# Output projection of a two-layer decoder step: its low parts and squares in a new order, and sixteen cached pages asked for ahead of the sliding branch's rows

## The chip, the core and the metric

The kernel runs on one core of a Trainium2 chip. The time is the device time of one execution in microseconds (us). The kernel before took 1862.92 us, the median of 3 runs (1859.42 to 1864.6). Everything is computed in one launch, in float32, most matmuls as products of float32 split in two parts.

## The reference, cut to what matters

Two groups of tokens share the weights: a prompt of 512 tokens, and 8 sequences of 4 new tokens each (32 tokens), with cached keys and values. All 544 tokens pass through 2 layers. Cut to the stages that the change touches:

```python
def window_attn(q, kv, q_pos, k_pos): ...        # sliding branch: the last 512 positions
def nsa_cmp_sel(q, cm, sb, q_pos): ...           # compressed branch, and 16 selected blocks of 64

def trunk_layer(x, c, pos, conv_buf, attend, recur, lw):
    ...
    q = rope(a_q...)
    kv_c, kv_s, kv_w = make_kv(a_kc, pos), make_kv(a_ks, pos), make_kv(a_kw, pos)
    o_c, o_s, o_w, win_state = attend(q, kv_c, kv_s, kv_w)
    a_out = gate[0] * o_c + gate[1] * o_s + gate[2] * o_w
    h, mstate = recur(mq, mk, mv, ...)
    m_out = sigmoid(m_o) * rms(h)
    x = x + g1 * (concatenate([a_out, m_out]) @ wo)        # the output projection
    xn2 = rmsnorm(x, n2) * (1 + sc2) + sh2                 # needs the squares of all of x
    f, new_buf = conv_ffn(xn2, conv_buf, w_up, ...)
    return x + g2 * f, ...
```

For the 8 sequences, past_s = cache_sel_kv[l][page_table] is 8 pages of 128 positions a sequence (64 pages a layer, 128 KB each), and cache_win_kv[l] holds 512 positions a sequence (512 KB each). The window rows, moved on by 4 positions, are outputs too.

## The kernel before, in words

Every engine has one queue of instructions in program order. They meet at semaphores (`sig(...)`: a producer adds 1, a consumer waits for a count), and all of TensorE, VectorE, ScalarE and GpSimd meet twice a layer at a fence, the semaphore `stage_done`: each adds 1 and waits until all four have.

**Decode attention** (between fence 8 and fence 12). SyncE issues the loads in one queue. In `pages` (L545 and L546) it reads a page's number from on-chip memory and then issues the DMA of that page. The pages of sequences 0 to 5 go first. It then waits for `mx_t` (TensorE has turned the last gates, L970), issues the window rows of sequences 0 to 3 (L598), the 16 pages of sequences 6 and 7, and the window rows of sequences 4 to 7. TensorE handles this in six rounds (`ROUNDS`, four sequences and 512 positions each): selected blocks of sequences 0 to 3 (rounds 0, 1), of 4 to 7 (rounds 2, 3), window rows of 0 to 3 (round 4) and of 4 to 7 (round 5). In `turn_keys` (L1027) it transposes keys; VectorE and ScalarE copy them out of PSUM, `score` (L1039) multiplies them by the queries, and the softmax and the values (L1078) follow. Where the pages of sequences 6 and 7 are turned is the second half of round 2. GpSimd waits for each half of the window rows and then stores them to the output (`put`, L2421), 8 stores a half; later it loads the recurrent state (L2487), and after VectorE has added to that state (`state_added`, L2227) it stores it by four pairs of DMAs (L2421 and L2499). It adds to `stage_done` after the last of these.

**Output projection** (after fence 12). `w_out` is loaded into `slab[0]` (output columns 0 to 511) and `slab[1]` (512 to 1023). ScalarE copies a slab, rounded, to `hiO` (`split_out`, L1579), and VectorE leaves the remainder in the slab (`low_out`, in place, L1721). The activations are split in the same way (`hiX` by ScalarE at L1593, the remainder `xnT` by VectorE). TensorE takes 8 chunks of 128 output columns. A chunk is 48 matmuls at L1192 (8 slices of the contraction, three products, two halves of the tokens). VectorE adds each chunk to the residual stream (`residual`, L2259 to L2264), ScalarE squares it (`square`, L1327), and TensorE sums the squares (`norm_sum`, L636): those of chunk 0 after the matmuls of chunk 1, and so on. Three pairs of PSUM banks hold chunks, so chunk c waits until chunk c-3 has been added.

VectorE's order there is: the remainder of `slab[0]`, the fence, 8 remainders of the activations, the remainder of `slab[1]`, the remainder of the first slice of the FFN's up weights (`split_w(0, 0)`, `slab[2]`), and only then the 8 additions. ScalarE's is: `hiX`, the copy of `slab[1]`, a wait for `slab[2]` and `split_w(0, 0)` (L1601), and then the 8 squares. After the last chunk the norm's root is taken and the FFN starts with the slice that `split_w(0, 0)` has prepared.

Of the kernel before, what the change touches and what calls it, by code (L numbers as in the profile page):

```python
# [125 lines left out]
def trunk_program(nc, A, O):  # L126
# [10 lines left out]
    with ctx:  # L137
# [197 lines left out]
        sig = Signal  # L335
# [30 lines left out]
        def slab_loads(stage, i, L, j=0):  # L366

            s, m = i % NSLAB, PARTS[stage]
            return L * (16 * dmas[s]) + j * (16 * m) + 16 * (first_dma[stage, s] + m * (i // NSLAB + 1))
# [118 lines left out]
        def x_at(k):  # L488

            return k + 1 if k < 4 else k + 2  # L490
        d_hi, d_lo = sig("weights_high", 2 + 2 * (NG + 1)), sig("weights_low", 2 + 2 * (NG + 1))
        i_hi, i_lo, i_lo0 = sig("input_weights_high", N_SLAB_IN), sig("input_weights_low", N_SLAB_IN - 1), sig("first_input_weights_low", 4)
        y_acc, y_add = sig("down_accumulated", 8 * (NG + 1)), sig("down_added", 8 * (NG + 1), credit=2)
        ul_t, ul_c = sig("tail_transposed", 6), sig("tail_copied", 6)
# [23 lines left out]
        def _(sp):  # L518
# [22 lines left out]
            for L in range(DEPTH):  # L541
# [50 lines left out]
                for b in range(6):  # L592
                    if b % 2 == 0:
                        sp.wait_ge(mod_t.sem, mod_t.at(mod_last(L, (1, 2, 0)[b // 2]) + 1))
                    pages(spg[b], sel_pool, b, spg_in[b // 2])
                sp.wait_ge(mx_t.sem, mx_t.at(4, L))
                for b in range(NB):
                    sp.dma_start(wpg[b].rearrange("p i c -> p (i c)"),  # L598
                                 A["cache_win_kv"][L][b].rearrange("(p i) a k d -> p (i a k d)", i=4)).then_inc(wpg_in[b // 4], 16)
                    if b == 3:  # L600
                        for c in (6, 7):
                            pages(spg[c], sel_pool, c, spg_in[c // 2])
                for i in range(2):
                    cols = slice(512 * i, 512 * i + 512)
                    load("out", i, [(sl(i, 8, 512)[:, 4:8, :], wout[L, :, 4:8, cols])] +
# [20 lines left out]
        def _(pe):  # L626
# [72 lines left out]
            for L in range(DEPTH):  # L699
# [477 lines left out]

                for c in range(8):
                    i = c // 4
                    if c % 4 == 0:  # L1180
                        pe.wait_ge(d_lo.sem, d_lo.at(i + 1, L))
                    if c >= 3:
                        pe.wait_ge(o_add.sem, o_add.at(c - 2, L))
                    cc = 128 * (c % 4)
                    lo = slab[i][:, :].rearrange("p (k n) -> p k n", k=8)
                    for k in range(KC):
                        if c == 0:
                            pe.wait_ge(x_lo.sem, x_lo.at(X_OUT + k + 1, L))
                        wh, wl = fr(hiO[i][:, k, cc:cc + 128]), fr(lo[:, k, cc:cc + 128])
                        for n, (wt, x) in enumerate(((wh, hiX), (wh, xnT), (wl, hiX))):  # L1190
                            for b in range(2):
                                ins = mm(ps[2 * (c % 3) + b][:, 0:HALF], wt, fr(x[:, k, HALF * b:HALF * b + HALF]),  # L1192
                                         start=k == 0 and n == 0, stop=k == KC - 1 and n == 2)
                                if c == 4 and k == 0 and n == 0 and b == 0:
                                    ins.then_inc(slab_out[0], 1)
                    ins.then_inc(o_acc.sem, 1)
                    if c:
                        norm_sum(2 * L + 1, c - 1, frees=1 if c == 7 else None)
                    if c == 5:
                        history()  # L1200
# [45 lines left out]
                def down(n_k, g=0, last=False):  # L1246

                    pe.wait_ge(h_lo.sem, h_lo.at(n_k + 4 * g, L))
                    pe.wait_ge(d_lo.sem, d_lo.at(4 + 2 * g, L))
                    lo = slab[1][:, :].rearrange("p (k n) -> p k n", n=D)  # L1250
                    for c in range(8):
                        pe.wait_ge(y_add.sem, y_add.at(c - 1 + 8 * g, L))
                        bank = (0 if last else 4) + 2 * (c % 2)
                        for k in range(n_k):
                            wh, wl = fr(hiD[:, k, 128 * c:128 * c + 128]), fr(lo[:, k, 128 * c:128 * c + 128])
                            for n, (wt, x) in enumerate(((wh, hiH), (wh, hid), (wl, hiH))):
                                for b in range(2):
                                    ins = mm(ps[bank + b][:, 0:HALF], wt, fr(x[:, k, HALF * b:HALF * b + HALF]),  # L1258
                                             start=k == 0 and n == 0, stop=k == n_k - 1 and n == 2)
                                    if last and c == 0 and k == 0 and n == 0 and b == 0:  # L1260
                                        ins.then_inc(slab_out[2], 1)
                        ins.then_inc(y_acc.sem, 1)
                        if last:
                            if c == 0:
                                pe.wait_ge(y_add.sem, y_add.at(8 * g, L))
                            if c < 6:
                                tail_rows(c)
                            if c >= 2:
                                norm_sum(2 * L + 2, c - 2)
                    pe.drain().then_inc(slab_out[1], 1)  # L1270
                    if last:
                        norm_sum(2 * L + 2, KC - 2)
                        norm_sum(2 * L + 2, KC - 1)
                        spread(2 * L + 2)
# [43 lines left out]
        def _(act):  # L1318
# [54 lines left out]
            for L in range(DEPTH):  # L1373
# [226 lines left out]
                        act.wait_ge(g_acc.sem, g_acc.at(cd - 1, L))  # L1600
                    A_(fr(hiU[:, q % 2, :, :, :]), src[:, :, :, cc:cc + 128], ACT.Copy).then_inc(w_hi.sem, 1)  # L1601

                act.wait_ge(slab_in[2], slab_loads("ffn", 2, L))
                split_w(0, 0, False)
                for c in range(8):
                    act.wait_ge(o_add.sem, o_add.at(c + 1, L))
                    square(2 * L + 1, c)
                root(2 * L + 1)

                def u_chunk(s, cd):  # L1610
# [60 lines left out]
        def _(dve):  # L1671
# [91 lines left out]
            for L in range(DEPTH):  # L1763
# [476 lines left out]
                state_added(4)  # L2240
                dve.wait_ge(d_out.sem, d_out.at(1, L))
                cp(xnT[:, 0:4, SEQ:TT], ps[6][:, 0:128].rearrange("p (g t) -> p g t", g=AG))
                state_added(5)

                def low_out(i):
                    dve.wait_ge(d_hi.sem, d_hi.at(i + 1, L))
                    low(slab[i][:, :].rearrange("p (k n) -> p k n", k=8), hiO[i]).then_inc(d_lo.sem, 1)

                low_out(0)
                dve.drain().then_inc(stage_done, 1)  # L2250
                dve.wait_ge(stage_done, stage_end(12, L))

# [13 lines left out]
                for k in range(KC):  # L2266
                    dve.wait_ge(x_hi.sem, x_hi.at(X_OUT + k + 1, L))
                    low(xnT[:, k, :], hiX[:, k, :]).then_inc(x_lo.sem, 1)
                low_out(1)

                def split_w(q, cd):
                    src = slab[(2, 0)[q % 4 // 2]][:, :].rearrange("p (k h n) -> p k h n", k=8, h=2)
# [1 line left out]
                    dve.wait_ge(w_hi.sem, w_hi.at(cd + 1, L))  # L2274
                    low(src[:, :, :, cc:cc + 128], hiU[:, q % 2, :, :, :]).then_inc(w_lo.sem, 1)

                split_w(0, 0)
                norm_scales(112 + 8 * L, 32)
                for c in range(8):
                    dve.wait_ge(o_acc.sem, o_acc.at(c + 1, L))  # L2280
                    residual(c, ps[2 * (c % 3)], ps[2 * (c % 3) + 1], 16 + c).then_inc(o_add.sem, 1)
                    drain()
                    if c == 6:
                        dve.wait_ge(cv_t.sem, cv_t.at(1, L))
                        cp(convS[:, :, :].rearrange("p c n -> p (c n)"), ps[7][:, 0:16 * FC])
                        dve.wait_ge(win_kept, 3 * L + 2)
                        V.memset(up[:, :, 0:2], 0.0)
# [264 lines left out]
```

## Time and profile before

| what | value |
|---|---|
| median of 3 runs | 1862.92 us (1859.42 to 1864.6) |
| the profiled execution's own time | 1863.74 us |
| its span in the trace | 1861.6 us |
| mean granted TensorE clock | 0.941 of full speed |
| TensorE busy | 1712.3 us (92%) |
| VectorE, ScalarE, GpSimd busy | 916.4 us (49%), 610.9 us (33%), 193.0 us (10%) |

TensorE is busy nearly all the time, so that what matters is where it stands still, and where it runs at the lower clock. A row of the timeline gives start and length of a group of instructions, and in brackets how long the engine had been idle and what released it. The chain of waits follows the end of the kernel back through what released what. SPq is SyncE's queue of DMA issues, L636 a line of kernel.py.

### The profile page before, as it was taken

The numbers are of one execution on the slowest core, as the hardware profiler recorded it, in microseconds if no ns is written. First come the engines' busy times: TensorE is split into PE (matmuls) and PEld (weight loads), VectorE is DVE, ScalarE is ACT, GpSimd is POOL, SyncE is SP. The second block draws the span as 40 slices with busy tenths as digits, with TensorE's granted clock in tenths as the row PEclk, the third lists the DMA queues.
The fourth block names the chain that finished last, engine by engine and source line by source line (L and its number), as shares of the span: only waits on it lengthen the run. The fifth ranks groups of instructions, "written<-read, shape, count | busy, mean of one in ns | idle before, by whom it ended". The sixth has DMA issues, their size and how long they took to land.

```text
span 1861.6 us, 37154 instructions
## 1 busy us (share of the span) xinstructions
PE 1712.3 (92%) x14719; PEld 1537.6 (83%) x14719; DVE 916.4 (49%) x2362; ACT 610.9 (33%) x1165; POOL 193.0 (10%) x312
## 2 busy tenths in 40 slices
PE   5899999976989999999989999897788999999996
PEld 4899875555889999999989997645588999999995
DVE  2444434645355645555463343474534655545643
ACT  2422225633133324224152212563323422412313
POOL 1001003433000000000000100153300000000001
PEclk9899978987989999999999997898888999999998
DMA  8335368379212222221123535635831222321201
GB/s 294 118 99 179 99 234 267 109 229 210 59 46 91 91 91 90 90 70 65 49 83 90 178 101 192 213 98 163 218 79 46 91 91 71 110 76 60 90 23 53
DMA packets 154291, 218.97 MB, mean 118 GB/s; under 512 B 11722, under 2 KB 112394, under 8 KB 153964
## 3 DMA queue, kind: packets, MB, share of 16 engines
q1 hardware_dynamic: 145872, 197.12, 33.3%
q0 software_dynamic: 8288, 20.04, 4.1%
q8 instruction: 89, 1.46, 0.3%
q14 instruction: 42, 0.34, 0.1%
HBM read 200.45 MB, written 16.68 MB: 117 GB/s over the span
## 4 chain that ended last, share of the span: by engine, by line
PE 80%; SPq 5%; DMA 5%; DVE 4%; ACT 3%; issue 2%; POOL 0%; DVEq 0%; ACTq 0%
PE ps L1232 27%; PE ps L1258 14%; PE ps L803 13%; PE ps L1192 4%; DMA slab<-in_w_up 4%; PE ps L677 3%; SPq L545 2%; SPq L546 2%; PE ps L848 1%; PE ps L914 1%; PE ps L884 1%; PE ps L789 1%; PE ps L798 1%; PE ps L797 1%; PE ps L929 1%
## 5 line engine op out<-in xcount | busy, mean ns | idle before, releaser
L1232 PE MATMUL ps<-work_r,big_r 128*128 128x272 f32 x1344 | 279.2, 289 | 5.6 <-issue 5.3
L1232 PE MATMUL ps<-work_r,slab_r 128*128 128x272 f32 x1344 | 278.5, 288 | 0.0
L1232 PE MATMUL ps<-xnT_r,big_r 128*128 128x272 f32 x1344 | 276.5, 287 | 0.0
L1232 PEld LDWEIGHTS ps<-work_r,big_r 128*128 128x128 f32 x1344 | 210.1, 188 | 8.1 <-issue 8.1
L803 PE MATMUL ps<-slab_r,work_r 128*128 128x256 f32 (+1 forms) x976 | 213.3, 285 | 0.0
L1232 PEld LDWEIGHTS ps<-xnT_r,big_r 128*128 128x128 f32 x1344 | 211.7, 188 | 0.0
L1232 PEld LDWEIGHTS ps<-work_r,slab_r 128*128 128x128 f32 x1344 | 210.6, 188 | 0.0
L1721 DVE TENSOR_TENSOR slab_r<-slab,big_r 128x2048 fp32r<-128x2048 f32 (+2 forms) x72 | 168.9, 2349 | 59.3 <-ACT big_r L1601 51.6
L803 PEld LDWEIGHTS ps<-slab_r,work_r 128*128 128x128 f32 x976 | 163.3, 191 | 2.7 <-issue 2.5
L1619 ACT ACTIVATE big<-big,work 128x560 f32<-128x560 f32 x44 | 33.6, 764 | 371.0 <-DVE big L2311 371.0
L1258 PE MATMUL ps<-side_r,big_r 128*128 128x272 f32 x704 | 148.3, 292 | 4.9 <-DVE big_r L1721 4.9
L1258 PE MATMUL ps<-big_r 128*128 128x272 f32 x704 | 146.2, 289 | 0.0
L1258 PE MATMUL ps<-side_r,slab_r 128*128 128x272 f32 x704 | 146.1, 289 | 0.0
L2259 DVE TENSOR_TENSOR work<-ps,modT 128x32 f32<-128x32 f32 x112 | 21.4, 191 | 252.1 <-PE ps L1258 180.6
L2421 POOL DMA_DIRECT2D out<-work x32 | 18.2, 574 | 1073.4 <-ACT work L1657 815.2
L1258 PEld LDWEIGHTS ps<-side_r,big_r 128*128 128x128 f32 x704 | 111.1, 190 | 7.7 <-DVE big_r L1721 5.4
L1258 PEld LDWEIGHTS ps<-big_r 128*128 128x128 f32 x704 | 111.5, 190 | 0.0
L1258 PEld LDWEIGHTS ps<-side_r,slab_r 128*128 128x128 f32 x704 | 111.0, 190 | 0.0
L1601 ACT ACTIVATE big_r<-slab 128x2048 fp32r<-128x2048 f32 x44 | 84.3, 1917 | 65.3 <-PE ps L1232 52.9
L803 PE MATMUL ps<-work_r 128*128 128x256 f32 (+1 forms) x336 | 96.4, 287 | 0.0
L803 PE MATMUL ps<-work_r,xnT_r 128*128 128x256 f32 (+1 forms) x336 | 94.1, 280 | 0.0
L803 PE MATMUL ps<-slab_r,xnT_r 128*128 128x256 f32 x320 | 90.8, 284 | 0.0
(447 smaller groups left out, 3232.6 us busy)
## 6 DMA issues: line engine op xcount, KB each, us to landing
slab<-in_w_mod SPq DMA_DIRECT2D x23, 2048.0 KB, 9.1
slab<-in_w_up SPq DMA_DIRECT2D x44, 1024.0 KB, 7.5
slab<-in_w_in SPq DMA_DIRECT2D x20, 1024.0 KB, 5.6
slab<-in_w_down SPq DMA_DIRECT2D x20, 1024.0 KB, 5.9
slab<-in_cache_cmp_kv SPq DMA_DIRECT2D x128, 128.0 KB, 2.0
slab<-in_cache_sel_kv SPq DMA_DIRECT2D x96, 128.0 KB, 2.0
big<-in_cache_win_kv SPq DMA_DIRECT2D x16, 512.0 KB, 5.1
out<-big POOLq DMA_DIRECT2D x16, 448.0 KB
```

The costliest lines, as they stand in the source:

```text
L545: pg = sp.value_load(pages_sb[0:1, NPG * b + p:NPG * b + p + 1], min_val=0, max_val=N_PHYS - 1)
L546: sp.dma_start(dst[:, p, :], src[bass.ds(pg + L * N_PHYS, 1)].squeeze(0)).then_inc(sem, 16)
L677: ins = mm(bank[32 * q:32 * q + 32, 0:128], cT[:, k, :], wv[:, k, 128 * q:128 * q + 128], start=k == 0, stop=k == KC - 1, tile_position=(0 ...
L789: ins = mm(ps[t][:, 0:cw], x, fr(wt[:, k, :]), start=k == 0 and m == 0, stop=k == KC - 1 and m == 2)
L803: ins = mm(ps[n % 4][:, 0:cw], x, fr(wt[:, k, :]), start=k == 0 and m == 0, stop=k == KC - 1 and m == 2)
L1192: ins = mm(ps[2 * (c % 3) + b][:, 0:HALF], wt, fr(x[:, k, HALF * b:HALF * b + HALF]), start=k == 0 and n == 0, stop=k == KC - 1 and n == 2)
L1232: ins = mm(ps[2 * half + b][:, 0:HALF], wt, fr(x[:, k, HALF * b:HALF * b + HALF]), start=k == 0 and n == 0, stop=k == KC - 1 and n == 2)
L1258: ins = mm(ps[bank + b][:, 0:HALF], wt, fr(x[:, k, HALF * b:HALF * b + HALF]), start=k == 0 and n == 0, stop=k == n_k - 1 and n == 2)
L1601: A_(fr(hiU[:, q % 2, :, :, :]), src[:, :, :, cc:cc + 128], ACT.Copy).then_inc(w_hi.sem, 1)
L1619: A_(cv[:, s, 0:UPW - 2], cv[:, s, 0:UPW - 2], ACT.Silu, bias=cbias[:, s:s + 1]).then_inc(u_si.sem, 1)
L1721: return tt(fr(dst), dst, fr(hi).bitcast(F), ALU.subtract)
L2259: tt(tmp.rearrange("p (b t) -> p b t", b=NB), hi[:, SEQ - HALF:HALF].rearrange("p (b t) -> p b t", b=NB), bc(gs, 2, NT), ALU.mult)
```

## The change

Three things are edited.

- SyncE: the 16 pages of sequences 6 and 7 are issued before all eight window rows (before: after the first four).
- The remainder of `w_out` is made in eight pieces of 128 columns instead of two of 512. Only the first stands ahead of the fence, and ahead of the last `state_added`. Three follow the activations, two each follow the additions of chunk 0 and chunk 1. TensorE waits for a piece ahead of every chunk; the counts of `weights_low` are moved by 6 for this.
- `split_w(0, 0)` goes on ScalarE behind the square of chunk 4, and on VectorE behind the addition of chunk 5.

```diff
@@ block.sync
                 sp.wait_ge(mx_t.sem, mx_t.at(4, L))
+                for c in (6, 7):
+                    pages(spg[c], sel_pool, c, spg_in[c // 2])
                 for b in range(NB):
                     sp.dma_start(wpg[b]...).then_inc(wpg_in[b // 4], 16)
-                    if b == 3:
-                        for c in (6, 7):
-                            pages(spg[c], sel_pool, c, spg_in[c // 2])
@@ block.tensor
-                    if c % 4 == 0:
-                        pe.wait_ge(d_lo.sem, d_lo.at(i + 1, L))
+                    pe.wait_ge(d_lo.sem, d_lo.at(c + 1, L))
@@ block.scalar
-                act.wait_ge(slab_in[2], slab_loads("ffn", 2, L))
-                split_w(0, 0, False)
                 for c in range(8):
                     act.wait_ge(o_add.sem, o_add.at(c + 1, L))
                     square(2 * L + 1, c)
+                    if c == 4:
+                        act.wait_ge(slab_in[2], slab_loads("ffn", 2, L))
+                        split_w(0, 0, False)
@@ block.vector
+                def low_out(i, cols):
+                    dve.wait_ge(d_hi.sem, d_hi.at(i + 1, L))
+                    low(slab[i]...[:, :, cols], hiO[i][:, :, cols]).then_inc(d_lo.sem, 1)
+
+                low_out(0, slice(0, 128))
                 state_added(5)
-                low_out(0)
                 dve.drain().then_inc(stage_done, 1)
@@
                     low(xnT[:, k, :], hiX[:, k, :]).then_inc(x_lo.sem, 1)
-                low_out(1)
+                for c in range(1, 4):
+                    low_out(0, slice(128 * c, 128 * c + 128))
@@
-                split_w(0, 0)
                 norm_scales(112 + 8 * L, 32)
                 for c in range(8):
                     residual(c, ...).then_inc(o_add.sem, 1)
                     drain()
+                    for n in ((0, 1), (2, 3))[c] if c < 2 else ():
+                        low_out(1, slice(128 * n, 128 * n + 128))
+                    if c == 5:
+                        split_w(0, 0)
```

VectorE's queue around fence 12 and behind it, before (the wait for `stage_done` is the fence; `slab_r<-slab,big_r` is a remainder of weights, `out_accumulated` a finished chunk):

```order
L2242 COPY xnT<-ps 128x4x32 [waits dec_out]
L2227 TENSOR_TENSOR work<-work,ps 128x2x129 [waits dec_state_sums]
L1721 TENSOR_TENSOR slab_r<-slab,big_r 128x4096 [waits weights_high]
L1721 TENSOR_TENSOR xnT_r<-xnT,work_r 128x544 [waits inputs_high,stage_done]
L1721 TENSOR_TENSOR xnT_r<-xnT,work_r 128x544 [waits inputs_high] x7
L1721 TENSOR_TENSOR slab_r<-slab,big_r 128x4096 [waits weights_high]
L1721 TENSOR_TENSOR slab_r<-slab,big_r 128x16x128 [waits up_w_high]
L1744 SCALAR_TENSOR_TENSOR scale_n<-modT,colsA 128x72
L2259 TENSOR_TENSOR work<-ps,modT 128x32 [waits out_accumulated]
```

and in the changed kernel (its line numbers are lower by one here):

```order
L2241 COPY xnT<-ps 128x4x32 [waits dec_out]
L1720 TENSOR_TENSOR slab_r<-slab,big_r 128x8x128 [waits weights_high]
L2226 TENSOR_TENSOR work<-work,ps 128x2x129 [waits dec_state_sums]
L1720 TENSOR_TENSOR xnT_r<-xnT,work_r 128x544 [waits inputs_high,stage_done]
L1720 TENSOR_TENSOR xnT_r<-xnT,work_r 128x544 [waits inputs_high] x7
L1720 TENSOR_TENSOR slab_r<-slab,big_r 128x8x128 [waits weights_high] x3
L1743 SCALAR_TENSOR_TENSOR scale_n<-modT,colsA 128x72
L2258 TENSOR_TENSOR work<-ps,modT 128x32 [waits out_accumulated]
```

A remainder of 4096 columns ahead of the fence became one of 1024, and it now precedes the last state addition; behind the fence the addition of chunk 0 no longer has the wait for `up_w_high` (the split of the up weights) ahead of it.

ScalarE's queue from the copy of `slab[1]` on, before:

```order
L1579 ACTIVATE big_r<-slab 128x4096 [waits slab1_loaded]
L1601 ACTIVATE big_r<-slab 128x2048 [waits slab2_loaded]
L1327 ACTIVATE big<-xT 128x544 [waits out_added] x2
L1327 ACTIVATE big<-xT 128x544 [waits norm_sums_spread,out_added] x6
L1332 ACTIVATE rstd<-rstd 128x136 [waits norm_var_inverse_scaled]
```

and in the changed kernel:

```order
L1577 ACTIVATE big_r<-slab 128x4096 [waits slab1_loaded]
L1325 ACTIVATE big<-xT 128x544 [waits out_added] x2
L1325 ACTIVATE big<-xT 128x544 [waits norm_sums_spread,out_added] x3
L1599 ACTIVATE big_r<-slab 128x2048 [waits slab2_loaded]
L1325 ACTIVATE big<-xT 128x544 [waits norm_sums_spread,out_added] x3
```

The wait for the load of `slab[2]` moved from ahead of all squares to behind five of them.

## Rows read from the trace of the kernel before

**Rows 1.** The page: the chain's shares by engine

```profile
PE 80%; SPq 5%; DMA 5%; DVE 4%; ACT 3%; issue 2%; POOL 0%; DVEq 0%; ACTq 0%
```

**Rows 2.** Chain of waits, layer 0's output projection (start, length, what)

```profile
439.75 34.16 DMA slab<-in_w_up
...
473.94 1.93 ACT big_r L1601
...
475.89 2.29 DVE slab_r L1721
...
480.66 7.73 PE ps L1192 x48
...
488.76 6.23 PE ps L1192 x48
```

**Rows 3.** Chain of waits, layer 1, the same chunk

```profile
1370.87 8.42 PE ps L1192 x48
```

**Rows 4.** Timeline of TensorE: first matmul, and first sum of squares of both layers

```profile
461.61 0.79 PE L1192 MATMUL ps<-work_r,big_r 128*128 128x272 f32 x2 [6.11 <-DVE xnT_r L1721]
...
480.22 0.44 PE L636 MATMUL ps<-big,shape_constants 128*32 128x136 f32 x8 [3.54 <-ACT big L1327]
...
1370.19 0.68 PE L636 MATMUL ps<-big,shape_constants 128*32 128x136 f32 x8 [4.96 <-ACT big L1327]
```

**Rows 5.** TensorE by microsecond: stretch, length, busy, clock, DMA share, GB/s

```profile
482.00:483.00 1.00, 1.00 (x6) 0.50 0.00 0
```

**Rows 6.** Timeline of VectorE around fence 12, layer 0

```profile
454.08 0.29 DVE L2242 COPY xnT<-ps 128x128 f32<-128x128 f32 x1 [0.88 <-PE ps L1115]
455.14 0.42 DVE L2227 TENSOR_TENSOR work<-work,ps 128x258 f32<-128x258 f32 x1 [0.77 <-PE ps L1105]
455.48 4.42 DVE L1721 TENSOR_TENSOR slab_r<-slab,big_r 128x4096 fp32r<-128x4096 f32 x1
460.74 5.17 DVE L1721 TENSOR_TENSOR xnT_r<-xnT,work_r 128x544 fp32r<-128x544 f32 x8 [0.84 <-ACT work_r L1593]
```

**Rows 7.** Timeline of GpSimd around fence 12, layers 0 and 1

```profile
455.86 0.69 POOL L2421 DMA_DIRECT2D out<-work  x1 [3.65 <-DVE work L2227]
...
459.26 0.69 POOL L2499 DMA_DIRECT2D out<-work  x1
...
1348.72 0.69 POOL L2499 DMA_DIRECT2D out<-work  x1
```

**Rows 8.** Timeline of SyncE's queue, layer 0

```profile
385.78 1.85 SPq L598 DMA_DIRECT2D big<-in_cache_win_kv  x4
388.73 19.51 SPq L546 DMA_DIRECT2D big<-in_cache_sel_kv  x16
408.28 1.86 SPq L598 DMA_DIRECT2D big<-in_cache_win_kv  x4
```

**Rows 9.** Line L545, 385 to 412 us: ns min/median/max, first and last start

```profile
L545 SPq TENSOR_LOAD <-pages_sb x16: 265/272/1626, 387.7 to 407.2; - x16
```

**Rows 10.** Timeline of TensorE: rounds 2 (layers 0, 1) and 5 (layer 0)

```profile
410.06 1.09 PE L1027 MATMUL ps<-shape_constants,big 128*128 128x128 f32 x8 [1.78 <-DMA big<-in_cache_sel_kv]
...
421.81 1.07 PE L1027 MATMUL ps<-shape_constants,big 128*128 128x128 f32 x8 [0.93 <-ACT work L1545]
...
1300.10 1.09 PE L1027 MATMUL ps<-shape_constants,big 128*128 128x128 f32 x8 [1.43 <-DMA big<-in_cache_sel_kv]
```

**Rows 11.** Timeline of GpSimd, layer 0: stores of the window rows, loads of state

```profile
395.83 4.23 POOL L2421 DMA_DIRECT2D out<-big  x8 [3.77 <-issue]
416.64 4.16 POOL L2421 DMA_DIRECT2D out<-big  x8 [16.58 <-DMA big<-in_cache_win_kv]
428.46 2.79 POOL L2487 DMA_DIRECT2D work<-in_state_mlstm_C  x4 [7.66 <-PE ps L1039]
```

**Rows 12.** Engines by stretch: length, busy of five, clock, DMA share, GB/s

```profile
388.00:392.00 4.00, 4.00 (x76) 3.15 (x76) 1.30 (x10) 0.87 (x5) 3.98 (x9) 0.66 0.99 367
...
420.00:424.00 4.00, 3.08 (x27) 1.79 (x25) 2.70 (x4) 2.27 (x4) 0.80 (x2) 1.00 0.98 305
```

More of the change, by code:

```diff
@@ L490, in x_at @@
             return k + 1 if k < 4 else k + 2
-        d_hi, d_lo = sig("weights_high", 2 + 2 * (NG + 1)), sig("weights_low", 2 + 2 * (NG + 1))
+        d_hi, d_lo = sig("weights_high", 2 + 2 * (NG + 1)), sig("weights_low", 8 + 2 * (NG + 1))
         i_hi, i_lo, i_lo0 = sig("input_weights_high", N_SLAB_IN), sig("input_weights_low", N_SLAB_IN - 1), sig("first_input_weights_low", 4)
@@ L1248, in down @@
                     pe.wait_ge(h_lo.sem, h_lo.at(n_k + 4 * g, L))
-                    pe.wait_ge(d_lo.sem, d_lo.at(4 + 2 * g, L))
+                    pe.wait_ge(d_lo.sem, d_lo.at(10 + 2 * g, L))
                     lo = slab[1][:, :].rearrange("p (k n) -> p k n", n=D)
@@ L2242, in _ @@
                 cp(xnT[:, 0:4, SEQ:TT], ps[6][:, 0:128].rearrange("p (g t) -> p g t", g=AG))
+                def low_out(i, cols):
+                    dve.wait_ge(d_hi.sem, d_hi.at(i + 1, L))
+                    low(slab[i][:, :].rearrange("p (k n) -> p k n", k=8)[:, :, cols], hiO[i][:, :, cols]).then_inc(d_lo.sem, 1)
+                low_out(0, slice(0, 128))
                 state_added(5)
-                def low_out(i):
-                    dve.wait_ge(d_hi.sem, d_hi.at(i + 1, L))
-                    low(slab[i][:, :].rearrange("p (k n) -> p k n", k=8), hiO[i]).then_inc(d_lo.sem, 1)
-                low_out(0)
                 dve.drain().then_inc(stage_done, 1)
```

## The prediction, made before the changed kernel was run

> **What bounds the kernel now.** I began with the page: the chain that ended last is TensorE for 80% [rows 1], so an edit pays where TensorE stands still or runs slowly. I then read the chain of waits through the output projection, and after it TensorE's timeline for every idle time there.
>
> The chain leaves TensorE for the load of the first up weights, which lands at 473.9 us; then follow ScalarE's copy, VectorE's remainder until 478.2, and chunk 0's addition and square [rows 2]. TensorE has done chunks 0 and 1 by then and stands still before it can sum chunk 0's squares, 3.54 us in layer 0 and 4.96 us in layer 1 [rows 4]. Nothing that it waits for needs the up weights: they only stand ahead in two queues. Behind the pause TensorE's granted clock is 0.50 for some microseconds [rows 5], that is 1.2 of 2.4 GHz, so the next chunk takes 7.73 and 8.42 us in place of 6.23 [rows 2, 3].
>
> The second place is fence 12, which was passed at about 460 us. VectorE reaches it at 455.48 + 4.42 = 459.90 [rows 6]. GpSimd's last issue ends at 459.26 + 0.69 = 459.95 [rows 7], and only then does it add to the fence. They tie. In layer 1 GpSimd's last issue ends at 1349.41 [rows 7].
>
> The third is round 2 of the decode attention: TensorE waits 1.78 us and 1.43 us for the pages of sequences 6 and 7 [rows 10]. SyncE issues these behind four window rows (1.85 us), and takes 19.51 us over them, the last at 408.2 [rows 8].
>
> **Squares and up-weight split.** The order of events afterwards, in layer 0 and in today's times: TensorE ends chunk 1 at 480.22 - 3.54 = 476.7, so chunk 0 ends 6.23 us earlier, at 470.4. VectorE is done with the activations at 460.74 + 5.17 = 465.9 [rows 6]. It then has three pieces of 1024 columns. No row has that shape. The nearest are 2.29 us for 2048 columns, cut the same way [rows 2], and 4.42 for 4096 whole [rows 6]; the difference is 2.13 for 2048, so 1.1 to 1.2 by proportion, and 2.29 as the upper bound (a piece as dear as one of twice the size). I take 1.2. The pieces end at 467.1, 468.3 and 469.5, and chunk 1 needs the first of them at 470.4. Addition and square of chunk 0 take from 478.24 to 480.2 today, about 2 us, and end at 472.5, 4 us before they are needed. Even with 2.29 a piece they end at 475. So the pause goes whole: 3.54 + 4.96 = 8.50 us. With it goes the slow chunk: (7.73 - 6.23) + (8.42 - 6.23) = 3.69 us, since nothing interrupts TensorE between chunks 0 and 1 any more. Sum 12.19; bounds: 8.50 if the lower clock comes anyway at another place, 12.5 with the slower sums beside it.
>
> What is late next? The four pieces of slab 1 stand behind additions 0 and 1: 4 x 1.2 (9.2 at the bound) within two chunks of 6.23, and chunk 4 needs the first of them only three chunks later. The up weights are split behind square 4, after 495 us, when they have long landed; VectorE's 2.29 stand between additions 5 and 6, in a gap of one chunk. Nothing of this reaches TensorE. Chunk 4's release of slab 0 moves earlier with everything else.
>
> **The remainder ahead of the fence.** It shrinks from 4.42 to 1.2, but GpSimd hides all of this gain: its six issues (three pairs, 455.86 to 459.95 [rows 7]) begin 0.30 us after the last state addition, which ended at 455.56 [rows 6]. That addition now stands behind the piece. The copy ends at 454.37, the piece follows until about 455.5, and the addition starts at 455.45 instead of 455.14. The fence comes 0.3 us later, 0.6 for both layers; with a piece of 2.29 it is 1.4 a layer, 2.8 in all. With the pieces free it would be zero.
>
> A page has a rule on this spot. The Trainium skill, SBUF — State Buffer, says in the warning on DVE blocking DMA that the descriptors of a DMA issued by GpSimd are written through ports that it shares with VectorE, so that some VectorE operations hold it up. A shorter remainder could then speed up GpSimd's issues too. The rows don't show that: each issue takes 0.69 us beside the long remainder.
>
> **Pages ahead of the window rows.** SyncE starts on the pages at once, 1.9 us earlier. Today the last issue ends at 408.24 [rows 8] and TensorE goes on 1.8 us later [rows 10]. 1.9 us earlier is just in time for its wish, 410.06 - 1.78 = 408.28. A second gain is likely: reading a page's number takes 272 ns in the median and up to 1626 [rows 9], and inside this loop GpSimd stores the first window rows (395.83 to 400.06 [rows 11]), which now comes behind all pages. I count two long reads less, 2.7 us: the last page is issued by 403.6 and has landed by 405.5. The waits of 1.78 and 1.43 go either way.
>
> What is late next are the window rows: the second half. Eight rows of 512 KB (4.2 MB) now go out from 403.7. At the 367 GB/s of the first half today [rows 12] the first half arrives near 410.3, before round 4. The second half is read while GpSimd stores the first (2 MB); the stores alone ran at 305 GB/s [rows 12]. I let the stores' data begin near 411.7, a microsecond behind their issue, when 1.5 MB are still to be read. Reading at about half rate, 0.165 MB/us, they arrive near 421.2. Round 5 wants them at 421.81 - 1.78 = 420.0 [rows 10]. So layer 0 keeps about 0.4 of 1.78; layer 1, whose copies ran a little faster, I give the whole 1.43. Together 1.8 us, with bounds of 3.2 (reads not slowed) and -3 (reads wait until the 4.2 MB and the 2 MB have all gone, 6.2 / 0.305 = 20.4 us after 404.4, that is 424.8, which costs 4.8 - 1.78 = 3.0 in layer 0; in layer 1 I count nothing then). Behind it GpSimd must be free for the state's load at 428.46 [rows 11]: its second stores end near 425.7, or 429 at the bound.
>
> Here a rule speaks against the change. The Trainium skill, DMA: Bandwidth & Descriptors, Queues, rings and completion order, says that each DMA engine goes round-robin between queues that have work, a packet at a time. By it stores and reads share, and the full rate is not to be had while both run. No row shows large reads and stores together, so this is open until the changed kernel's trace; by the rule the gain would be nearer to zero than to 3.2.
>
> **Sum.** -12.2 (pause and clock), +0.6 (fence), -1.8 (pages) = -13.4 us. The profiled execution took 1863.74 us with a span of 1861.6, 0.8 above the median of 1862.92. From its own time the sum gives 1850.3, from the median 1849.5. I predict 1850, with 1845 to 1855 as this case's own range: 3 us from the pages, 2 from the pieces, and 2 from where after the fence the clock rises.
>
> **Rivals.**
> - *The fence falls too.* If GpSimd's issue spans are rough and it adds to the fence well before VectorE today, the shorter remainder pays. VectorE would then be through at 455.9 instead of 459.9, at most 4 us a layer and 8 in all: 1863.7 - 12.2 + 0.6 - 1.8 - 8 = 1842.3. For it: VectorE's end at 459.90 would fit as the releaser just as well. Against it: issues run in the queue's order, and both layers show the tie. 10%.
> - *Only the pause goes.* The low clock, which comes and goes in steps, reappears behind the fence or before the norm, and the pages give nothing net: -8.5 + 0.6 = -7.9, 1855.8. For it: the clock moves in steps and at times that no row ties to a single wait, and the two layers lost different amounts (1.50 and 2.19). Against it: behind chunk 0 nothing would stop TensorE. 18%.
> - *The pieces are dear (slower).* If a piece of 128 columns out of 512 costs as much as the whole 4.42, the fence comes 3.5 us later, three pieces end at 479.2, chunk 0 is squared at 481.4, later than today, and additions 1 and 2 stand behind two pieces (8.8 us) each against a chunk of 6.23. TensorE then pauses three times, about 1.2 + 3.5 + 3.5 us with 3 us of low clock: +15 a layer, 1893. It costs more than it gives from about 3 us a piece. The 2.29 us of twice the size, cut the same way, speak against it. 3%.
> - *The change doesn't do what it says:* the pages aren't what round 2 waits for, and the window rows arrive late, the bound of +3 above. The projection's gain stays: 1863.7 - 11.6 + 3 = 1855. 7%.
>
> My forecast has 62%.
>
> **Range and chances.** A measurement of this kernel can tell about 0.3%, 5.6 us, from no change, so the border is 1857.3. The forecast, the first and the last rival lie below it, the second by 1.5 us only. Faster 0.91, same 0.06, slower 0.03. The range reaches from 1843 (part of the way to the first rival) to 1857.
>
> **What the changed kernel's profile would show.** TensorE's sum of chunk 0's squares without an idle time, and all eight chunks of the projection within 0.2 us of 6.23, once the clock has risen. A piece of 1.1 to 1.3 us. Fence 12 released by GpSimd, its six issues starting some 0.3 us later after the copy than now. No idle time in the second half of round 2, and perhaps a new one of up to 2 us at round 5, released by the window rows' DMA. I am wrong if the fence moves by microseconds, if chunks wait for `weights_low`, if the low clock returns in the middle of the projection, or if round 5 waits for more than 3 us.

## The result, and the profile after

The changed kernel takes 1840.33 us, the median of 9 runs (1834.96 to 1850.55). The kernel before, in 9 runs, takes 1859.42 (1853.3 to 1864.6). The ratio is 0.9907, 95% interval 0.9883 to 0.9932: 17.3 us faster, with 12.6 to 21.8 possible. Run again on another occasion beside other kernels (`changed_again`) the ratio was 0.9926 (0.9902 to 0.9949), 13.8 us. The forecast was 1850, with 1843 to 1857 as its range. The direction was right, the time 3 us below the range.

The page of the changed kernel, its span and the shares of the chain, against [rows 1]:

```profile
span 1836.7 us, 37174 instructions
PE 84%; DVE 5%; DMA 3%; ACT 3%; SPq 2%; issue 2%; POOL 1%; DVEq 0%; ACTq 0%
```

Whole spans mislead here. From the last gate transposes (L970) to the first matmul of the FFN, the stretch that the change touches, I took seven landmarks in both traces, each the start of an instruction (L969, L1210 and so on in the changed kernel; for the fence, ScalarE's first instruction behind it). They bound six stretches. In us, layer 0 / layer 1:

| stretch | before | after | difference |
|---|---|---|---|
| gate transposes to importance matmul | 13.96 / 13.54 | 11.09 / 10.87 | -2.87 / -2.67 |
| to the last keys turned (round 5) | 26.29 / 26.42 | 27.75 / 25.35 | +1.46 / -1.07 |
| to the product with the recurrent state | 12.86 / 12.91 | 15.25 / 16.49 | +2.39 / +3.58 |
| to VectorE's copy out of d_out | 17.41 / 16.79 | 16.24 / 18.16 | -1.17 / +1.37 |
| to the release of fence 12 | 5.90 / 5.90 | 4.29 / 4.59 | -1.61 / -1.31 |
| to the FFN's first matmul | 71.98 / 73.40 | 66.14 / 66.11 | -5.84 / -7.29 |
| sum | 148.40 / 148.96 | 140.76 / 141.57 | -7.64 / -7.39 |

That is 15.0 us. The spans differ by 24.9; the other 9.9 us lie where nothing was edited. Two rows show this, each from the FFN of layer 0 to the attention of layer 1 (length, busy time of TensorE, its loads, VectorE, ScalarE, GpSimd, then the clock). Before:

```profile
532.00:1270.00 738.00, 715.38 (x5837) 651.60 (x5839) 384.60 (x1007) 255.75 (x500) 61.77 (x96) 0.96 0.31 100
```

and after:

```profile
523.00:1255.00 732.00, 707.53 (x5840) 647.10 (x5841) 384.25 (x1006) 255.79 (x500) 61.64 (x96) 0.97 0.31 101
```

TensorE has the same matmuls to within a few records, and 7.9 us less busy time with them at a mean granted clock of 0.97 instead of 0.96. In all 13 traces of this study the time outside the table's stretch is between 1554 and 1567 us, and it goes with the time that the clock was at its lower level there. Both profiles of the changed kernel are at the low end (1554.3 and 1555.1), with 104 and 98 us at the lower level against 105 to 133 in the other eleven. The runs of one kernel spread over 5 to 24 us, and the second of these profiles is of the fastest of its six runs, so I read it as chance. That is not shown: two of two at the low end may also be an effect of the change.

**The projection.** The chain of the changed kernel in layer 0, which answers to [rows 2]:

```profile
457.83 14.33 PE ps L1190 x96
472.16 0.37 PE ps L635 x8
472.53 6.22 PE ps L1190 x48
478.75 0.37 PE ps L635 x8
479.12 6.21 PE ps L1190 x48
```

Chunks 0 and 1 run on without a break, the sum of chunk 0's squares follows at once, and each later chunk takes 6.22 us. The pause of [rows 4] and the slow chunk are gone. A piece of the remainder, and an activation's remainder (ns, smallest, median, largest):

```profile
L1720 DVE TENSOR_TENSOR slab_r<-slab,big_r x8: 1215/1219/1226, 452.1 to 474.7; 128x1024 fp32r<-128x1024 f32 x8
L1720 DVE TENSOR_TENSOR xnT_r<-xnT,work_r x8: 717/718/726, 457.0 to 461.4; 128x544 fp32r<-128x544 f32 x8
```

1.22 us, where I took 1.2.

**The fence.** Timeline of VectorE, ScalarE and GpSimd in the changed kernel, which answers to [rows 6, 7]:

```profile
451.91 0.29 DVE L2241 COPY xnT<-ps 128x128 f32<-128x128 f32 x1 [0.88 <-PE ps L1114]
452.12 1.22 DVE L1720 TENSOR_TENSOR slab_r<-slab,big_r 128x1024 fp32r<-128x1024 f32 x1
453.25 0.42 DVE L2226 TENSOR_TENSOR work<-work,ps 128x258 f32<-128x258 f32 x1
...
456.20 4.48 ACT L1591 ACTIVATE work_r<-xnT 128x544 fp32r<-128x544 f32 x8 [2.56 <-POOLq L2505]
...
453.96 0.69 POOL L2424 DMA_DIRECT2D out<-work  x1 [3.42 <-DVE work L2226]
...
457.35 0.69 POOL L2502 DMA_DIRECT2D out<-work  x1
```

ScalarE goes on at 456.20, released by GpSimd's queue, and GpSimd's last issue only starts at 457.35. So the queue had passed its addition to the fence while four of the six issues, as the trace shows them, were begun, and two were still to come. The span of such an issue is not the time at which the queue moves on.

Before the change VectorE was the last, not both. The trace of the kernel before had a row that says so, in either layer, and I had not read it: ScalarE leaves the fence released by VectorE's queue.

```profile
459.98 4.48 ACT L1593 ACTIVATE work_r<-xnT 128x544 fp32r<-128x544 f32 x8 [4.17 <-DVEq L2250]
...
1349.45 4.48 ACT L1593 ACTIVATE work_r<-xnT 128x544 fp32r<-128x544 f32 x8 [4.17 <-DVEq L2250]
```

The times at which `stage_done` was counted up, which that trace also holds, are 455.56, 455.85, 458.08 and 459.96. The last is VectorE's. The third lies 2.5 us behind the last state addition, as GpSimd's does in the changed kernel (453.67 to 456.18), so GpSimd had been at the fence 1.9 us before VectorE. In layer 1 the two are 1347.84 and 1349.43.

**The pages.** SyncE's queue, and its reads of page numbers, against [rows 8, 9]:

```profile
384.32 17.75 SPq L546 DMA_DIRECT2D big<-in_cache_sel_kv  x16
402.12 3.98 SPq L600 DMA_DIRECT2D big<-in_cache_win_kv  x8
```

```profile
L545 SPq TENSOR_LOAD <-pages_sb x16: 264/268/275, 383.6 to 401.0; - x16
```

The long reads are gone, as forecast. TensorE's waits in layer 0 (start, length, in brackets idle time and releaser), against [rows 10]:

```profile
392.67 0.64 PE L1123 MATMUL ps<-work,shape_constants 128*128 128x32 f32 x2 [1.66 <-DVE work L2129]
...
403.77 1.09 PE L1026 MATMUL ps<-shape_constants,big 128*128 128x128 f32 x8 [0.56 <-DMA big<-in_cache_sel_kv]
...
410.76 1.60 PE L1026 MATMUL ps<-shape_constants,big 128*128 128x128 f32 x8 [1.91 <-DMA big<-in_cache_win_kv]
...
435.67 3.32 PE L1089 MATMUL ps<-work 64*32 64x129 f32 x64 [4.02 <-DVEq L2185]
```

The new wait for window rows is at round 4, 1.91 us here and 1.19 in layer 1; round 5 waits for them only in layer 1, 1.00 us. The first of these waits had been, in the kernel before, the longest of the decode attention, and I had not followed it up. Before, TensorE and then VectorE:

```profile
397.52 0.64 PE L1124 MATMUL ps<-work,shape_constants 128*128 128x32 f32 x2 [4.54 <-DVE work L2130]
...
394.99 0.17 DVE L2122 RECIPROCAL work<-work 128x2 f32<-128x2 f32 x1 [3.35 <-DMA rows_bc<-in_mlstm_norm_g]
```

VectorE waited for GpSimd's small loads of gain rows, which landed late beside 2 MB of window rows. With the window rows moved back TensorE's wait shrinks from 4.54 to 1.66 us and, in layer 1, from 4.49 to 1.93. What follows takes it back: round 2 still waits 0.56 us, round 4 waits for the window rows, and the recurrent state comes late: 10.6 us from GpSimd's first issue (425.07) to TensorE's product at 435.67, where before it was 436.67 - 428.46 = 8.2 [rows 11]. The size of this last loss varies: in the other profiles of kernels with pages first and the state's load in its place, the stretch to the state's product takes 12.8 to 19.0 us. Together with the stretch ahead of it, it is steadier: 41.7 to 44.0 us with the pages first, 38.4 to 41.6 with the old order (`gains_late` left out).

Rates, with stores and reads together in the second row (length, busy times, clock, DMA share, GB/s):

```profile
403.00:411.00 8.00, 4.97 (x38) 2.93 (x35) 4.43 (x6) 2.94 (x5) 0.00 (x0) 1.00 0.99 366
411.00:416.00 5.00, 4.45 (x24) 2.21 (x22) 1.21 (x2) 1.20 (x2) 4.22 (x8) 0.66 1.03 414
```

Reads alone ran at 366 GB/s, as in [rows 12] (367). Reads and stores together reached 414 in sum, by their queues 267 and 147, more than the 330 that I had assumed.

### The profile page after: what moved, and what is told of

The parts are those of the page before. It is cut to its first block, busy times and chain, and to the rows that moved or that the text cites. A ratio compares the mean times of both kernels' runs of the same rounds, so it can differ in the third digit from the quotient of the medians.

```text
span 1836.7 us, 37174 instructions
## 1 busy us (share of the span) xinstructions
PE 1696.9 (92%) x14719; PEld 1525.4 (83%) x14719; DVE 917.9 (50%) x2374; ACT 610.7 (33%) x1165; POOL 192.6 (10%) x312
## 3 DMA queue, kind: packets, MB, share of 16 engines
q8 instruction: 89, 1.46, 0.3%
## 4 chain that ended last, share of the span: by engine, by line
PE 84%; DVE 5%; DMA 3%; ACT 3%; SPq 2%; issue 2%; POOL 1%; DVEq 0%; ACTq 0%
PE ps L1230 28%; PE ps L1256 15%; PE ps L802 13%; PE ps L1190 6%; PE ps L676 3%; PE ps L913 2%; PE ps L928 2%; PE ps L847 2%; PE ps L883 1%; PE ps L788 1%; PE ps L797 1%; PE ps L796 1%; DMA work<-in_state_mlstm_C 1%; DMA big<-in_cache_win_kv 1%; PE ps L1210 1%
## 5 line engine op out<-in xcount | busy, mean ns | idle before, releaser
L1720 DVE TENSOR_TENSOR slab_r<-slab,big_r 128x2048 fp32r<-128x2048 f32 (+1 forms) x84 | 170.2, 2036 | 48.3 <-ACT big_r L1599 44.2
```

The costliest lines, as they stand in the source:

```text
L1720: return tt(fr(dst), dst, fr(hi).bitcast(F), ALU.subtract)
```

## The experiments

Differences in time are to the kernel before, run beside each. "Stage sum" is that of the table: before 297.4 us, changed 282.3.

**proj_only**: everything but the SyncE edit.

```diff
-                for c in (6, 7):
-                    pages(spg[c], sel_pool, c, spg_in[c // 2])
                 for b in range(NB):
                     sp.dma_start(wpg[b]...)
+                    if b == 3:
+                        for c in (6, 7):
+                            pages(spg[c], sel_pool, c, spg_in[c // 2])
```

> The change without its SyncE edit: window rows and pages are issued as before. Theory A (the changed kernel's trace: the pause and slow chunk go, 5.8 and 7.3 us from first chunk to the FFN, and the fence also falls, 1.6 to 1.9 us a layer, because GpSimd's sequencer passes its last issues before their spans end): about -16 us against before, and fence 12 within 4.5 us of the copy out of d_out. Theory B (as predicted: the fence is held by the ends of GpSimd's issue spans): -11.6 us, the fence 6 us behind the copy.

Measured: 1841.59 us, ratio 0.9922 (0.9893 to 0.995), -14.5 us. Stage sum 282.6, within 0.3 us of that with the SyncE edit. Fence 4.29 and 4.59 us behind the copy, to the digit as in the changed kernel, released by GpSimd's queue. Theory A holds, with a gain 1.5 us under its 16.

**pages_only**: the kernel before with the SyncE edit of the change alone.

> Before, with only the pages issued ahead of the window rows. Theory A: three shifts cancel. TensorE's wait for VectorE ahead of the importance matmul (4.5 us) shrinks by 2.9 and 2.7 us because the gain rows land sooner; round 2 loses its wait and round 4 gets one of 1 to 2; the recurrent state lands 2.4 and 3.6 us later behind the stores of the second half. Sum +1 us, within 0.3% of before. Theory B: the edit gives the surplus of the measured result over the forecast, 4 to 6 us faster.

Measured: ratio 1.0007 (0.9982 to 1.0032), no difference. The surplus does not come from the pages. The first four rows of the table come to 140.3 us for both layers, before to 140.2. The stage sum is even 303.4, 6 us more: the importance wait shrinks to 1.67 us in both layers, but the wait for the recurrent state grows to 7.2 and 7.4, and, which I had not said, the pause in the projection from 3.5 and 5.0 to

```profile
480.22 0.68 PE L635 MATMUL ps<-big,shape_constants 128*32 128x136 f32 x8 [9.11 <-ACT big L1326]
```

and 9.7: the up weights still land at 473.9, and TensorE is simply there sooner.

**split_only**: the kernel before, with only the split of the up weights moved.

```diff
-                act.wait_ge(slab_in[2], slab_loads("ffn", 2, L))
-                split_w(0, 0, False)
                 for c in range(8):
                     act.wait_ge(o_add.sem, o_add.at(c + 1, L))
                     square(2 * L + 1, c)
+                    if c == 4:
+                        act.wait_ge(slab_in[2], slab_loads("ffn", 2, L))
+                        split_w(0, 0, False)
@@ block.vector
-                split_w(0, 0)
                 norm_scales(112 + 8 * L, 32)
                 for c in range(8):
                     residual(c, ...)
                     drain()
+                    if c == 5:
+                        split_w(0, 0)
```

> Before, with only the split of the first up weights moved (ScalarE behind square 4, VectorE behind addition 5); the remainders of w_out stay two whole ones, the first ahead of the fence. Theory A: the pause of 3.5 and 5.0 us goes and with it the slow chunk, -12 us, but the fence stays 5.9 us behind the copy. Theory B (the pause needs the pieces too, since the whole remainder of slab 1 still stands ahead of addition 0): a pause of 1 us or more stays before the first sum of squares, and the gain is under 8 us.

Measured: 1846.01 us, ratio 0.994 (0.9915 to 0.9964), -11.2 us. Stage sum 283.6, fence 5.90 behind the copy, no pause in either layer. VectorE ends the whole remainder of slab 1 in time for addition 0:

```profile
466.14 4.43 DVE L1722 TENSOR_TENSOR slab_r<-slab,big_r 128x4096 fp32r<-128x4096 f32 x1 [2.10 <-ACT big_r L1579]
470.48 0.23 DVE L1745 SCALAR_TENSOR_TENSOR scale_n<-modT,colsA 128x72 f32<-128x72 f32 x1
470.62 0.18 DVE L2260 TENSOR_TENSOR work<-ps,modT 128x32 f32<-128x32 f32 x1
```

The move of one split carries 13.8 of the 15.0 us in the stage. The rest of the change adds little although its fence falls 2.9 us earlier, because part of that goes back. TensorE leaves the fence sooner and does more of chunk 0 before the clock rises. In layer 0 the granted clock rose at 462.8, 4.7 us behind the fence, and in the changed kernel at 462.4, 6.2 us behind it. Chunks 0 and 1 take

```profile
459.73 13.70 PE ps L1192 x96
```

instead of the 14.33 of the changed kernel.

**pieces_only**: the other half, the remainders cut into pieces, the split ahead of the squares.

```diff
+                low_out(0, slice(0, 128))
                 state_added(5)
-                low_out(0)
@@
-                low_out(1)
+                for c in range(1, 4):
+                    low_out(0, slice(128 * c, 128 * c + 128))
                 split_w(0, 0)
@@ after additions 0 and 1
+                    for n in ((0, 1), (2, 3))[c] if c < 2 else ():
+                        low_out(1, slice(128 * n, 128 * n + 128))
```

> Before, with only the remainders of w_out cut into pieces; the split of the up weights stays ahead of the squares, the pages where they were. Theory A: the fence comes 4.3 to 4.6 us behind the copy instead of 5.9, but the pause behind chunk 1 stays and grows by what the fence gave (the load of the up weights lands when it does): 1.3 to 1.6 us longer, so no gain in time. Theory B: the cut alone shortens the pause, since less stands ahead of addition 0, and is worth 2 us or more a layer.

Measured: ratio 1.0028 (0.9998 to 1.0058), no gain. Stage sum 298.9. The fence is at 4.29 and 4.59, and the pause is 6.90 and 10.62 us instead of 3.54 and 4.96. It grew by more than the fence gave, so the two sizes of theory A don't match, but its point does: a fence that falls earlier is worth nothing while the load of the up weights holds the squares.

**gains_late**: the kernel before, with VectorE's wait for the gain rows moved to where they are used.

```diff
-                dve.wait_ge(gst_in, L * 64 + 64)
                 dve.wait_ge(d_cexp.sem, d_cexp.at(1, L))
@@
+                dve.wait_ge(gst_in, L * 64 + 64)
                 tt(MOst, MOst, gst, ALU.mult)
```

> Before, with VectorE's wait for the gain rows (gst_in) moved from ahead of the block probabilities to the multiplication that uses them. Theory A (this wait is what the page edit shortened): TensorE's idle time of 4.5 us ahead of the importance matmul falls to about 1.7, but round 2's wait for the pages of sequences 6 and 7 grows by as much, since SyncE issues them no earlier: 1.8 and 1.4 become 4 to 4.5, and the time stays within 0.3%. Theory B (the wait shrinks for another reason, such as the missing reads of window rows beside it): the idle time stays at 4.5 us.

Measured: ratio 1.001 (0.9981 to 1.0038). TensorE in layer 0:

```profile
390.74 0.64 PE L1124 MATMUL ps<-work,shape_constants 128*128 128x32 f32 x2 [1.60 <-DVE work L2129]
...
407.08 1.97 PE L1027 MATMUL ps<-shape_constants,big 128*128 128x128 f32 x8 [5.43 <-DMA big<-in_cache_sel_kv]
```

Idle time of 1.60 instead of 4.54, and round 2 waits 5.43 and 5.00 instead of 1.78 and 1.43. The stage sum is 301.1. The wait was the gain rows', and pages are next in line behind it.

**state_first**: the changed kernel, with the state's loads ahead of the second half's stores.

```diff
+                keep_rows(0)
                 pool.wait_ge(d_s.sem, d_s.at(6, L))
                 ... four loads of the state ...
+                keep_rows(1)
```

(`keep_rows(half)` is the loop of stores of four sequences' window rows, which stood ahead of the wait for both halves.)

> The changed kernel, with GpSimd's loads of the recurrent state put ahead of its stores of the second half of the window rows. Theory A (the state's load waits behind those stores, in one queue and on the same DMA engines): TensorE's wait ahead of the state's product falls from 4.0 and 6.2 us to 2.6 or less, 3 to 5 us in all, so about 3 to 5 us faster than the changed kernel. Theory B (the load is slow because of reads of w_out, or the stores now end so late that the copy of w_out, which waits for them, is late): no gain, or a wait of ScalarE ahead of the copy of slab 0.

Measured: 1842.62 us, ratio 0.9925 (0.9903 to 0.9947), no faster than the changed kernel. The stage sum is 280.2, 2.1 us less, which times that spread by 5 us and more can't confirm. The stretch to the state's product fell from 15.25 and 16.49 to 13.72 and 12.96 us, so the load did stand behind the stores. Of these 5.1 us 3.3 went back at the fence, 6.33 and 5.84 us behind the copy instead of 4.29 and 4.59, as theory B had it: ScalarE waits for w_out, which is now loaded beside the stores.

```profile
444.48 3.62 ACT L1577 ACTIVATE big_r<-slab 128x4096 fp32r<-128x4096 f32 x1 [5.40 <-DMA slab<-in_w_out]
...
448.13 1.23 DVE L1720 TENSOR_TENSOR slab_r<-slab,big_r 128x1024 fp32r<-128x1024 f32 x1 [1.95 <-ACT big_r L1577]
```

**fence_first**: the changed kernel, with GpSimd's addition to fence 12 ahead of its last three pairs of stores.

```diff
                 for s_ in range(2):
                     for q_ in range(2):
                         pool.wait_ge(ms_Cc.sem, ms_Cc.at(3 * q_ + 3, L))
+                        if s_ == 0 and q_ == 1:
+                            pool.sem_inc(stage_done, 1)
                         ... put(s_C ...), dma_start(s_n ...)
-                pool.sem_inc(stage_done, 1)
```

> The changed kernel, with GpSimd's addition to fence 12 put ahead of its last three pairs of stores (behind its wait for the last state addition). Theory A (GpSimd's queue holds the fence, some 2.3 us behind the last state addition): the fence falls to within 2.0 to 2.3 us of the copy out of d_out instead of 4.3 to 4.6, the next releaser is VectorE's drain, and the kernel is 4 to 5 us faster than the changed one. Theory B (the fence is held elsewhere and GpSimd's name in the trace is an inference): no change of that distance.

Measured: 1838.92 us, ratio 0.9899 (0.987 to 0.9928). The fence comes 1.84 us behind the copy in both layers, 2.45 and 2.75 us earlier. Stage sum 276.7, 5.6 less than the changed kernel. The chain around it:

```profile
453.55 0.29 DVE xnT L2241
453.84 1.13 DVE slab_r L1720
454.98 0.34 DVEq L2249
...
455.34 0.03 POOLq L2501
...
455.39 0.67 ACT work_r L1591
```

VectorE's drain ends at 455.32 and GpSimd's addition follows 0.05 us later, as both stand behind the last state addition (454.89 to 455.31). VectorE's piece, and no longer GpSimd's issues, sets the fence. In the changed kernel the fence was GpSimd's, about 2.5 us behind the state addition: theory A.

**combo**: state_first and fence_first together, the first piece behind the last state addition.

```diff
-                low_out(0, slice(0, 128))
                 state_added(5)
+                low_out(0, slice(0, 128))
```

> state_first with two edits more: GpSimd adds to fence 12 ahead of its last three pairs of stores, and the first remainder of w_out stands behind the last state addition. Theory A (in state_first the gain at the state's product, 1.5 and 3.5 us, went back at the fence, because the piece waited for ScalarE's late copy and the state addition and GpSimd's stores behind it): the fence waits for the piece alone, about 3.5 us behind the copy, and the sum from the last gate transposes to the FFN is 6 to 8 us less than in the changed kernel. Theory B: the late load of w_out sets the fence anyway, and the gain stays under 3 us.

Measured: 1835.91 us, ratio 0.9893 (0.9855 to 0.9931), with runs from 1830.81 to 1849.66. The profiled execution is one of the two longest (1848.45). Its stage sum is 279.6, 2.7 us less than the changed kernel's. In layer 1 the sum is 138.0 and the fence 3.79 us behind the copy, as in theory A. In layer 0 ScalarE waits 7.0 us for slab 0 of w_out, which puts the fence at 6.10, as in theory B, and then 12.5 us for slab 1. The square of chunk 0 stands behind that copy in ScalarE's queue, and the pause is back:

```profile
474.20 0.68 PE L635 MATMUL ps<-big,shape_constants 128*32 128x136 f32 x8 [5.94 <-ACT big L1325]
```

It is the fault that the change removed, with another load: work that doesn't need the data stands behind the wait for it. That the four shorter runs lacked this wait is a guess, as none was profiled, and what makes the load of slab 1 late was not settled.

**changed_again, fence_again, proj_fence**: the changed kernel and fence_first once more, and fence_first without the SyncE edit, on one chip.

> The changed kernel once more, beside the next two on one chip. By its stages (15 us less than before from the last gate transposes to the FFN, the rest of the kernel unchanged) it should be 15 us faster than before, ratio 0.992; if the 25 us between the two first profiles were real, 0.987.

> fence_first once more on the same chip: by its stages 5.6 us less than the changed kernel, ratio to before 0.989. If what the fence gave is lost behind it (a later load, the clock), no difference to the changed kernel.

> fence_first with pages and window rows issued as before the change. Theory A (the page edit moves waits and gives nothing net): within 2 us of fence_first, the idle time ahead of the importance matmul back at 4 to 5.5 us, round 2 waiting 2 to 2.7 us, the wait for the recurrent state back at 2.5 to 3 us. Theory B (the page edit is worth its own 1.8 us or more once the fence is free): 2 to 4 us slower than fence_first.

Measured: ratios 0.9926 (0.9902 to 0.9949), 0.9905 (0.9881 to 0.993) and 0.9912 (0.9885 to 0.9939); medians 1843.66, 1839.39 and 1843.82 us. Stage sums 283.2, 276.6 and 277.9. The fence's 1.84 us came back exactly, and proj_fence is within 1.3 us of fence_again in the stage: importance wait 4.9 and 5.0, round 2's 1.8 and 3.1, state's 2.9 and 3.9. In the times the step from the changed kernel to fence_first has the right sign twice (4.3 us here), but the intervals overlap. By the traces it beats the changed kernel by a known cause; by the measured times it is only not slower. Likewise proj_fence: its median is 4.4 us above fence_again's, which would be theory B, with intervals that overlap; theory A rests on the traces.

## Why the prediction was right or wrong

**Squares and up-weight split: right.** The forecast was -12.2 us; measured -13.1 (5.84 + 7.29). The pause and the slow chunk went, nothing took their place, and split_only shows that the moved split is the cause. Of the 0.9 us more, 0.8 lie in layer 0 (forecast 5.04, measured 5.84; layer 1 7.15 and 7.29). There chunk 0 took 9.0 us before and 8.3 after, since the clock rose 7.8 us behind the fence before and 6.2 after. The forecast had no term for this, and I can't say why it rose sooner.

**The remainder ahead of the fence: the step that failed.** I wrote "GpSimd hides all of this gain", and counted +0.6. Measured: -2.9 (1.61 + 1.31). The error was to read the end of GpSimd's last issue span as the time at which its queue reaches the fence. It got there at 458.08, 1.9 us before VectorE, and the trace before already named VectorE's queue as the releaser. What I had right is that the issues start 0.3 us later after the copy (2.05 us instead of 1.78) and that GpSimd holds the fence then. The two ends of 459.90 and 459.95 were a coincidence of this case, and both layers showed it because both run the same instructions. The rival "the fence falls too" had the mechanism, with 10% and 8 us; the size was a third of that, since GpSimd's queue does hold the fence next, 2.5 us behind the state addition in layer 0 and 2.8 in layer 1. fence_first shows it. The issues took 0.69 us each before and after, so the shorter remainder didn't speed them up.

**Pages ahead of the window rows: right in its parts, wrong in the sum.** Forecast -1.8, measured +1.0 (the first four rows of the table), and pages_only, proj_only and proj_fence show likewise that it is worth nothing within a microsecond or two. The short reads of page numbers came as thought. The new wait came at another place: I had the first half of the window rows land near 410.3, before round 4, and a wait at round 5. They landed near 410.8, but round 4 wanted them 1.91 us before that, having moved up with round 2. (The working for round 5 also slips: 421.2 is 1.2 us behind 420.0, which leaves 0.6 of 1.78, not 0.4.) I missed two things besides: the wait for the gain rows, 5.5 us in all, which this edit removes and gains_late traces to these rows; and the recurrent state's load behind the second half's stores, +6.0 in this profile, which I had looked at only for whether GpSimd would be free. The rule that the prediction cites from the Trainium skill, DMA: Bandwidth & Descriptors, Queues, rings and completion order, that each DMA engine goes round-robin between queues that have work, fits the trace: reads fell from 366 to 267 GB/s beside 147 of stores. It pointed the right way for the net, but what cancelled the gain was for the larger part the load of the state behind the stores.

**The sum, and the level.** By terms the forecast was -13.4, the stage measured -15.0, the ratios -17.3 and -13.8, with -13.4 inside both intervals. That the sum comes so near is luck in part: the fence gave 3.5 us more than forecast and the pages 2.8 less, and the two cancel. The miss of the time, 9.7 us below 1850, is made of four parts. The median before, 1862.92 of 3 runs, was 3.5 us above the 1859.42 of 9, and a forecast of a time inherits this. The stage gave 1.6 us more (3.5 from the fence, 0.9 from the squares, less 2.8 from the pages). The medians differ by 19.1 us, 4.1 more than the stage, which is not explained and was not there in changed_again (medians 14.5 us apart, stage sum 14.2 less than before). The rounding to 1850 is 0.5. Without the failed step on the fence the forecast would have been 1846.5, and a range of the same width around it would have reached down to 1839.5 and held the measurement. The range counted only the terms' bounds, not the spread of the level, which was 5 to 24 us from run to run.

## What to carry to other kernels

When a wait for data stands in a queue ahead of work that doesn't need the data, move the wait behind the work: one such move was worth 11 us here (split_only), and shortening the instructions around it was worth nothing until it had been made (pieces_only). Before calling a gain hidden by another engine, find a row in which that engine is the named releaser; a span that happens to end at the right time isn't one. When a large transfer is moved, list every small load of the stage and every store that is queued ahead of a later load, not only the transfer's own reader.

## What the runs showed of the hardware

- GpSimd's queue goes past its DMA issues before their spans end: its addition to the fence counted at 456.18 us, while the issues ahead of it in the queue are shown until 458.04.
- SyncE's reads of a page number took up to 1626 ns while GpSimd stored window rows, and at most 275 ns when these stores came after the reads, 16 reads each.
- Small loads issued by GpSimd (16 KB) landed in 5.4 us beside 2 MB of window rows, and in 2.2 us beside pages alone.
- Outside the edited stretch the time of nearly the same instructions varied between 1554 and 1567 us over 13 traces, and the time at the lower clock with it, from 98 to 133 us.
